# Where the weight tiles start: products of 256 columns with operands at other distances modulo 256 bytes

## The chip, the cores and the metric

The kernel runs on one core of one Trainium2 chip. The metric is the device time of one execution in microseconds. Three timed executions of the kernel before gave 1921.24, 1917.67 and 1925.44, so the median is 1921.24. The execution that the profiler recorded took 1927.16.

## The reference, cut to what matters

Everything is float32, with 256 tokens of x, 256 of a context, and 1024 features. Two blocks run one after the other. The first has a gated FFN (1024 to 2816 and back), attention of two kinds and a second gated FFN:

```python
def swiglu(x, w_gate, w_up, w_down):
    return (jax.nn.silu(x @ w_gate) * (x @ w_up)) @ w_down

h = swiglu(rmsnorm(x, ffn1_pre_g), ffn1_w_gate, ffn1_w_up, ffn1_w_down)
x = x + 0.5 * rmsnorm(h, ffn1_post_g)
qkv = rmsnorm(x, mix_pre_g) @ w_qkv          # then attention of 16 heads
x = x + rmsnorm(concat(o_na, o_dil) @ w_out, mix_post_g)
h = swiglu(rmsnorm(x, ffn2_pre_g), ffn2_w_gate, ffn2_w_up, ffn2_w_down)
x = x + 0.5 * rmsnorm(h, ffn2_post_g)
```

The second block has two layers. Each projects with w_in, mixes in three branches (Fourier, windowed attention, a gated recurrence), and ends with a squared-relu MLP:

```python
y = sum_n(sigmoid(gate_n) * (branch_n @ w_branch[l][n])) @ w_out[l]
x = x + mx[2] * y
x = x + mx[5] * (jnp.square(jax.nn.relu(h2 @ w_ff1[l])) @ w_ff2[l])
```

The first of the two layers works on x and the context together, 512 tokens; the last one updates x alone, 256 tokens.

## The kernel before, in words

The activations are kept with features on the partitions and tokens along the row, so a product takes a weight tile of 128 by 128 as its stationary operand and the activations of 256 tokens (or 512) as its moving one. Products are made to float32 accuracy out of three in the type float32r: each operand is split into a high and a low half, and high by high, high by low and low by high are added in PSUM. So 128 output columns with contraction over 1024 take 8x3 products.

The weights come as a stream of blocks of 128 by 1024, in the order in which TensorE uses them. SyncE loads block n into wr[n % 4]. ACT copies it, rounded, to wh (L451, `make_high`), and DVE or GpSimd subtracts the copy from the original into wl (L468, `make_low`). There are three buffers of wh and three of wl. TensorE reads them in `dense` and `dense_group` (L504, L508, L511) and in `three` (L596 to L604), where L599 is wh by the high half, L602 wh by the low half and L604 wl by the high half. A row of wh or wl holds 1024+64 elements. Where in the row a block starts is `past_line`'s answer for its first tile, in elements of 4 bytes; `Weights.tile` keeps it in `past`, and `halves_of` adds it to each address, for the copy, the subtraction and the product alike.

The buffers wr, wh, wl, X, HH and HL all start at 128 bytes modulo 256. Each tile's columns are 512 bytes further and each k of the activations 1024 or 2048, so within a weight the distance from the weights to the moving operand is one number modulo 256. The moving operands of w_qkv, the gates and ups, w_out, w_ff1_2 and two branches are in HH and HL, at 128; the third branch's are in OHH and OHL, at 128; those of the FFN down products are in NHH and NHL, at 96; those of w_out_2 in the last layer are in Y1, at 96; those of w_ff2_2 there in HID1, at 160. With a start of 16 elements (64 bytes) for HH and 8 (32 bytes) for NHH and Y1 the distance is 192 for all of them: 128-128-64 and 96-128-32 are both -64. `past_line` gives 0 for tiles of 512 columns, for w_in_2 and w_ff2_2, and for all weights of the first of the two layers. There the distance is 0, or 32 for w_ff2_2 in the last layer.

The order of work on TensorE is: FFN1 gate and up to 141 us, its down products to 206, w_qkv to 259, attention, w_out 314 to 337, FFN2 gate and up 341 to 477, its down products to 541; the first layer of the second block to 1409, all but small parts of it with 512 columns; the last layer to the end, with w_branch_2 from 1656 to 1709, w_out_2 to 1734, w_ff1_2 1737 to 1834 and w_ff2_2 after it. In the gate and up products of FFN2 short sums in plain float32 (L678) stand between the products; they belong to a norm of the context.

Of the kernel before, what the change touches and what calls it, by code (L numbers as in the profile page):

```python
# [23 lines left out]
REC_FILLS, OUT_FILLS = ((2, 2, 2, 2, 2, 2, 2), (3, 3, 3, 3, 3, 3, 3)), ((1, 1, 1), (1, 1, 1))  # L24
KB_ = 1024
ARENA = 96 * KB_ + 512
PAST = 16
HALF_D, HALF_T = 65, 130


# [141 lines left out]
def past_line(name, width):  # L172


    if width == 512 or name[0] in ("w_in_2", "w_ff2_2") or name[0].endswith("_2") and name[1] == 0:
        return 0
    return 8 if name[0] in ("ffn1_w_down", "ffn2_w_down", "w_out_2") else PAST


class Weights:  # L180
# [8 lines left out]
    def tile(self, name, k, cols, split=True):  # L189
        width = sum(b - a for a, b in cols)  # L190
        if self.col + width > 1024 or split != self.split:
            self.n, self.col, self.split = self.n + 1, 0, split
            self.kinds.append(split)
            self.past.append(past_line(name, width))
        c = self.col
        self.order.append((self.n, c, name, k, tuple(cols)))
        self.col += width
        self.fill[self.n] = self.col
        end = self.old is not None and self.old.fill[self.n] == self.col
        return self.n, c, self.col, end  # L200
# [3301 lines left out]
```

## Time and profile before

| | us |
|---|---|
| median of three runs | 1921.24 |
| the three runs | 1917.67 to 1925.44 |
| the profiled execution | 1927.16 |
| its span, first to last instruction | 1925.2 |
| TensorE busy in it | 1873.0 |
| weight loads on TensorE | 1661.5 |
| DVE, ACT, GpSimd busy | 1229.9, 944.9, 474.7 |

Products are pipelined: one that is shown as 276 ns long starts 113 ns after the one ahead of it. So the pace of TensorE is read from the starts in the timeline, and its busy time only tells that it had something in work.

### The profile page before, as it was taken

The numbers are of one execution on the slowest core, as the hardware profiler recorded it, in microseconds if no ns is written. First come the engines' busy times: TensorE is split into PE (matmuls) and PEld (weight loads), VectorE is DVE, ScalarE is ACT, GpSimd is POOL, SyncE is SP. The second block draws the span as 40 slices with busy tenths as digits, with TensorE's granted clock in tenths as the row PEclk, the third lists the DMA queues.
The fourth block names the chain that finished last, engine by engine and source line by source line (L and its number), as shares of the span: only waits on it lengthen the run. The fifth ranks groups of instructions, "written<-read, shape, count | busy, mean of one in ns | idle before, by whom it ended". The sixth has DMA issues, their size and how long they took to land.

```text
span 1925.2 us, 31215 instructions
## 1 busy us (share of the span) xinstructions
PE 1873.0 (97%) x12606; PEld 1661.5 (86%) x12606; DVE 1229.9 (64%) x1989; ACT 944.9 (49%) x1508; POOL 474.7 (25%) x328
## 2 busy tenths in 40 slices
PE   8999999999999999999999999999999999999999
PEld 8989988898998888786788888888897998798988
DVE  6888898779857853666663753354377847786410
ACT  6444447655457443426733531233265654765643
POOL 2211022000000000003344354555500000304887
PEclk9999999999999999999999999999999999999999
DMA  8987563576832212221123344466532333154554
GB/s 308 280 256 262 195 221 129 179 229 232 272 130 96 70 47 97 88 66 45 66 97 133 107 168 142 153 218 217 176 101 99 126 128 131 58 177 143 187 193 153
DMA packets 83951, 297.12 MB, mean 154 GB/s; under 512 B 9704, under 2 KB 12912, under 8 KB 83552
## 3 DMA queue, kind: packets, MB, share of 16 engines
q1 hardware_dynamic: 65600, 232.81, 35.9%
q0 software_dynamic: 16592, 58.79, 9.8%
q10 hardware_dynamic: 1616, 3.52, 0.5%
q8 instruction: 100, 1.64, 0.3%
q14 instruction: 43, 0.35, 0.1%
HBM read 294.02 MB, written 2.54 MB: 154 GB/s over the span
## 4 chain that ended last, share of the span: by engine, by line
PE 77%; DVE 12%; ACT 4%; issue 3%; DMA 3%; POOL 1%; DVEq 0%; SPq 0%; ACTq 0%; POOLq 0%
PE ps L604 20%; PE ps L599 20%; PE ps L602 19%; DVE wl L468 4%; PE ps L596 3%; ACT wh L451 2%; DMA wr<-wstream 2%; PE ps L598 1%; PE ps L2180 1%; DMA X<-wmod 1%; PE ps L1379 1%; PE ps L1277 1%; PE ps L1275 1%; PE ps L1280 1%; DVE HH L1133 1%
## 5 line engine op out<-in xcount | busy, mean ns | idle before, releaser
L599 PE MATMUL ps<-HH,wh 128*128 128x256 f32 (+1 forms) x2160 | 700.7, 324 | 4.6 <-ACT wh L451 3.7
L604 PE MATMUL ps<-HH,wl 128*128 128x256 f32 (+1 forms) x2160 | 688.1, 319 | 11.8 <-DVE wl L468 9.6
L602 PE MATMUL ps<-HL,wh 128*128 128x256 f32 (+1 forms) x2160 | 685.7, 317 | 0.0
L451 ACT ACTIVATE wh<-wr 128x1024 fp32r<-128x1024 f32 x440 | 459.6, 1053 | 331.0 <-PE ps L604 227.7
L468 DVE TENSOR_TENSOR wl<-wr,wh 128x1024 fp32r<-128x1024 f32 x301 | 366.9, 1223 | 192.0 <-ACT wh L451 191.5
L604 PEld LDWEIGHTS ps<-HH,wl 128*128 128x128 f32 x2160 | 408.5, 189 | 44.6 <-DVE wl L468 13.3
L599 PEld LDWEIGHTS ps<-HH,wh 128*128 128x128 f32 x2160 | 409.1, 189 | 41.4 <-issue 9.5
L602 PEld LDWEIGHTS ps<-HL,wh 128*128 128x128 f32 x2160 | 409.7, 190 | 30.4 <-issue 2.4
L468 POOL TENSOR_TENSOR wl<-wr,wh 128x1024 fp32r<-128x1024 f32 x139 | 337.1, 2428 | 208.7 <-ACT wh L451 207.7
L1534 POOL TENSOR_TENSOR s<-s,ST 128x512 f32<-128x512 f32 x56 | 57.3, 1039 | 656.9 <-DVE ST L1502 656.6
L1133 DVE CUSTOM_DVE_ANT_0 PROD<-WM,COND 128x1024 f32<-128x1024 f32 x104 | 127.6, 1241 | 1.3
L2940 DVE SCALAR_TENSOR_TENSOR X<-ps,MOD,X 128x256 f32<-128x256 f32 x60 | 26.9, 480 | 139.3 <-PE ps L604 139.0
L1106 POOL DMA_DIRECT2D WM<-wmod x68 | 37.5, 552 | 306.2 <-DVE MOD L1133 306.2
L599 PE MATMUL ps<-HIDH,wh 128*128 128x512 f32 (+1 forms) x272 | 102.6, 377 | 0.0
L604 PE MATMUL ps<-NHH,wl 128*128 128x256 f32 x352 | 99.4, 282 | 3.3 <-DVE wl L468 3.3
L604 PE MATMUL ps<-HIDH,wl 128*128 128x512 f32 (+1 forms) x272 | 102.4, 377 | 0.0
L602 PE MATMUL ps<-HIDL,wh 128*128 128x512 f32 (+1 forms) x272 | 102.4, 377 | 0.0
L599 PE MATMUL ps<-NHH,wh 128*128 128x256 f32 x352 | 98.6, 280 | 0.0
L602 PE MATMUL ps<-NHL,wh 128*128 128x256 f32 x352 | 98.6, 280 | 0.0
L3012 DVE TENSOR_TENSOR tm<-tm,ps 128x512 f32<-128x512 f32 (+1 forms) x64 | 35.4, 553 | 69.6 <-ACT tm L2993 69.6
L596 PE MATMUL ps<-HID,wh 128*128 128x512 f32 x224 | 77.7, 390 | 0.0
L2993 ACT ACTIVATE tm<-ps 128x512 f32<-128x512 f32 (+1 forms) x64 | 31.2, 488 | 81.7 <-PE ps L604 80.2
(314 smaller groups left out, 2968.6 us busy)
## 6 DMA issues: line engine op xcount, KB each, us to landing
wr<-wstream SPq DMA_DIRECT2D x440, 512.0 KB, 3.4
WM<-wmod POOLq DMA_DIRECT2D x68, 512.0 KB, 4.5
X<-wmod POOLq DMA_DIRECT2D x28, 512.0 KB, 6.6
NAB<-naskew POOLq DMA_DIRECT2D x16, 128.0 KB, 7.5
DILB<-dilskew POOLq DMA_DIRECT2D x8, 256.0 KB, 7.4
COND<-cond ACTq DMA_DIRECT2D x2, 1024.0 KB, 4.5
X<-xin SPq DMA_DIRECT2D x4, 256.0 KB, 5.6
HL<-cond ACTq DMA_DIRECT2D x1, 1024.0 KB, 8.2
```

The source lines that it names most:

```text
L451: ins = e.activation(self.halves_of(n, 0, 1024)[0], self.WR[n % NRAW][:, :], ACT.Copy)
L468: ins = e.tensor_tensor(wl, self.WR[n % NRAW][:, :], wh.bitcast(F32), ALU.subtract)
L596: e.matmul(out, wh, beside(xh, xl), start=i == 0, stop=False)
L599: e.matmul(out, wh, xh, start=i == 0, stop=False)
L602: e.matmul(out, wh, xl, start=False, stop=False)
L604: return e.matmul(out, wl, xh, start=False, stop=i == n_k - 1)
L1106: e.dma_start(self.mod_buffer(z, i), src).then_inc(self.mod_sem[i], 16)
L1133: ins = e.tensor_tensor_reduce(out=P, in0=self.mod_buffer(z, i), in1=S, scale=1.0, scalar=0.0, op0=ALU.mult, op1=ALU.add, accum_out=self.M ...
L1534: ins = e.tensor_tensor(sv, sv, bc(st[:, 4:4 + rows], 2, 512 // rows), ALU.mult)
L2940: ins = e.scalar_tensor_tensor(out=self.X[:, d, sl], in0=self.main.item(k)[:, sl], scalar=self.MOD[:, l, mod_i + d, c:c + 1], in1=self.X[: ...
L2993: e.activation(v, self.main.item(key)[:, 0:T], ACT.Relu).then_inc(*self.c("relu").mark((l, f)))
L3012: e.tensor_tensor(v, v, self.main.item(key)[:, 0:T], ALU.mult).then_inc(*self.c("sqr").mark((l, f)))
```

## The change

The constant PAST, 16 elements, becomes a table by the weight's name, and the exception for three names goes into it.

```diff
-PAST = 16
+PAST = dict(ffn1_w_gate=48, ffn1_w_up=48, ffn1_w_down=40, w_qkv=24, w_out=24, ffn2_w_gate=8, ffn2_w_up=8,
+            ffn2_w_down=0, w_branch_2=32, w_out_2=8, w_ff1_2=40)
@@ def past_line(name, width):
     if width == 512 or name[0] in ("w_in_2", "w_ff2_2") or name[0].endswith("_2") and name[1] == 0:
         return 0
-    return 8 if name[0] in ("ffn1_w_down", "ffn2_w_down", "w_out_2") else PAST
+    return PAST[name[0]]
```

With the places of the moving operands the distances become:

| weight | start before, after (bytes) | moving operand at | distance before, after |
|---|---|---|---|
| ffn1 gate, up | 64, 192 | 128 | 192, 64 |
| ffn1 down | 32, 160 | 96 | 192, 64 |
| w_qkv (q and k), w_out | 64, 96 | 128 | 192, 160 |
| ffn2 gate, up | 64, 32 | 128 | 192, 224 |
| ffn2 down | 32, 0 | 96 | 192, 224 |
| w_branch_2, last layer | 64, 128 | 128 | 192, 128 |
| w_out_2, last layer | 32, 32 | 96 | 192, 192 |
| w_ff1_2, last layer | 64, 160 | 128 | 192, 96 |

## Rows read from the trace of the kernel before

**Rows 1.** The page: busy time by engine, granted clock in 40 slices, last chain.

```profile
PE 1873.0 (97%) x12606; PEld 1661.5 (86%) x12606; DVE 1229.9 (64%) x1989; ACT 944.9 (49%) x1508; POOL 474.7 (25%) x328
...
PEclk9999999999999999999999999999999999999999
...
PE 77%; DVE 12%; ACT 4%; issue 3%; DMA 3%; POOL 1%; DVEq 0%; SPq 0%; ACTq 0%; POOLq 0%
```

**Rows 2.** Timeline of TensorE, FFN2 gate and up: start, duration (us), instruction.

```profile
383.17 0.28 PE L604 MATMUL ps<-HH,wl 128*128 128x256 f32 x1
...
385.89 0.28 PE L604 MATMUL ps<-HH,wl 128*128 128x256 f32 x1
```

**Rows 3.** Timeline of TensorE, FFN2 down.

```profile
484.54 0.28 PE L602 MATMUL ps<-NHL,wh 128*128 128x256 f32 x1
...
540.49 0.28 PE L604 MATMUL ps<-NHH,wl 128*128 128x256 f32 x1
```

**Rows 4.** Timeline of TensorE, w_in_2 in the last layer.

```profile
1551.92 0.28 PE L602 MATMUL ps<-HL,wh 128*128 128x256 f32 x1
...
1571.84 0.28 PE L604 MATMUL ps<-HH,wl 128*128 128x256 f32 x1
```

**Rows 5.** Timeline of TensorE, last output of w_ff2_2.

```profile
1910.99 0.28 PE L599 MATMUL ps<-HID,wh 128*128 128x256 f32 x1
...
1921.84 0.28 PE L599 MATMUL ps<-HID,wh 128*128 128x256 f32 x1
```

**Rows 6.** Timeline of TensorE, w_ff2_2 in the first layer, 512 columns.

```profile
1199.82 0.39 PE L599 MATMUL ps<-HIDH,wh 128*128 128x512 f32 x1
...
1201.86 0.39 PE L599 MATMUL ps<-HIDH,wh 128*128 128x512 f32 x1
```

**Rows 7.** Timeline of TensorE, FFN2 gate and up, around an L678 sum.

```profile
392.09 0.60 PE L678 MATMUL ps<-tm,CT 128*128 128x256 f32 x2
...
393.11 0.28 PE L604 MATMUL ps<-HH,wl 128*128 128x256 f32 x1
```

**Rows 8.** Windows on slow stretches: length, PE busy (count), clock, DMA, GB/s; sums: all 18, then by weight.

```profile
sum 294.69, PE 294.69; mean PE 16.37
...
sum 49.82, PE 49.82; mean PE 12.46
...
155.19:197.23 42.04, 42.04 (x359) 1.00 0.78 263
...
sum 16.26, PE 16.26; mean PE 5.42
...
317.54:337.09 19.55, 19.55 (x169) 1.00 0.74 265
...
386.55:392.09 5.54, 5.54 (x50) 1.00 0.55 164
...
sum 27.33, PE 27.33; mean PE 5.47
...
484.54:540.61 56.07, 56.07 (x479) 1.00 0.78 263
...
1686.18:1691.60 5.42, 5.42 (x49) 1.00 0.30 100
...
sum 78.20, PE 78.20; mean PE 39.10
```

**Rows 9.** L468 on DVE, FFN1 gate and up, then down: min/median/max ns.

```profile
L468 DVE TENSOR_TENSOR wl<-wr,wh x39: 1205/1221/1228, 19.0 to 136.9; 128x1024 fp32r<-128x1024 f32 x39
...
L468 DVE TENSOR_TENSOR wl<-wr,wh x23: 1216/1222/1228, 141.0 to 204.6; 128x1024 fp32r<-128x1024 f32 x23
```

**Rows 10.** Waits of the weight loads, 354 to 477 us: total, times, longest.

```profile
PEld ps L604 <- DVE wl L468: 5.5, 6, 1.1
```

**Rows 11.** Groups of instructions, 1747 to 1834 us: count, busy us, mean ns, idle before.

```profile
L468 POOL TENSOR_TENSOR wl<-wr,wh 128x1024 fp32r<-128x1024 f32 x29 | 69.7, 2408 | 86.5 <-ACT wh L451 86.5
```

**Rows 12.** Window on FFN1 gate and up, TensorE alone, columns as in rows 8.

```profile
20.00:141.00 121.00, 115.36 (x963) 1.00 0.92 277
```

## The prediction

> **What bounds the kernel now.** I read the page's busy line and its chain first [rows 1]: TensorE is busy 97% of the span and holds 77% of the chain that ended last, so in most stages its pace is the pace of the kernel. The change moves weight tiles in memory and adds or removes no instruction, so the question is whether the pace of one product depends on the place of its operands. A product's duration doesn't tell it, since products overlap; the distance from one start to the next in the timeline does. Where TensorE waits for nothing, four spacings are to be seen, and D is the distance in bytes from the weights to the moving operand, modulo 256:
>
> With D=192 there is a fast pace: in the second FFN's gate and up products, 24 products start between 383.17 and 385.89 us, 113.3 ns each [rows 2]. With the same D there is a slow one: in that FFN's down products, 475 between 484.54 and 540.49, 117.8 ns each [rows 3]. With D=0, in the last layer's w_in_2, 166 between 1551.92 and 1571.84, 120.0 ns each [rows 4]. With D=32, in the last outputs of w_ff2_2, 93 between 1910.99 and 1921.84, 116.7 ns each [rows 5]. Products of 512 columns at D=0 take 226.7 ns (9 between 1199.82 and 1201.86 [rows 6]), which is twice 113.3: there the distance costs nothing, and 113.3 looks like the floor for 256 columns. The clock isn't it: the page grants nine tenths or more of full speed in each slice of the span [rows 1], and 1.00, the level of 2.4 GHz, in the slow stretches [rows 8].
>
> So place matters, and at D=192 the pace has two values that hold for long stretches. What ends one is a break in the stream: behind the L678 sum that follows the product at 385.89 the pace is slow from 386.55 on [rows 2, 8], behind the same sum at 392.09 it is fast from 393.11 on [rows 7]. The slow one isn't bound to a weight.
>
> How much of it there is: 18 stretches of slow pace, found by going through the starts and shown by their sum, hold 294.69 us (the first sum of [rows 8]). A slow product costs 117.8-113.3=4.45 ns over the floor, 3.78% of its time, so all slow stretches together cost 11.1 us. That is the most that the floor can give back. They hold 294.69/0.11778=2502 products of the 4800 whose D changes (by the code, three products for each 128 columns of output and each k: gate and up 2x44x8x3=2112, down 2x8x22x3=1056, w_qkv's q and k 16x8x3=384, w_out 192, w_branch_2 in the last layer 3x8x4x3=288, w_ff1_2 in the last layer 32x8x3=768). The other 2298 are taken as fast. w_out_2 keeps 192, and products of 512 columns, w_in_2 and w_ff2_2 keep their places.
>
> **The change part by part.** No instruction, wait or DMA is added, removed or moved past a queue. The copies to wh (L451) and the subtractions to wl (L468) write the same bytes at another offset. Their cost I take at nothing: at offsets of 64 bytes in FFN1 and 32 in its down stage the median subtraction is 1221 and 1222 ns [rows 9].
>
> What is left is the pace at each new D, and no trace shows 64, 96, 128, 160 or 224. The bounds for each are the ends of the rows: 113.3 below and 120.0 above. Between them I choose by distance on the circle of 256 bytes, since the known rows fall with it: 120.0 at 0, 116.7 at 32, 113.3 or 117.8 at 64 (192 is 64 the other way round).
>
> First, w_ff1_2 (96), w_qkv and w_out (160) and w_branch_2 (128) come to lie further apart than 64, where I take the fast pace throughout. Their slow stretches now [rows 8]: w_ff1_2 78.20 us (two stretches), w_out 19.55, w_qkv 16.26 (three stretches), w_branch_2 5.42; together 119.43 us, times 3.78% is -4.5 us. Bounds: -4.5, or 1632 products at 120.0, which is 10.9-4.5=+6.4.
>
> Second, FFN1 goes to 64, the same distance as 192. I take no difference. Bounds: its slow stretches [rows 8], gate and up 49.82 (four of them) and down 42.04, gone: -3.5 us; all of its 1584 products at 120.0: +7.1.
>
> Third, FFN2 goes to 224, the distance of D=32, so 116.7 for all. Its down stage is slow now over 56.07 us [rows 8], 476 products that would gain 1.1 ns each, and 52 at the floor lose 3.3: -0.35 us. Its gate and up stage has 27.33 us slow (one stretch ahead of 361 us, and four of 47 products behind L678), 232 products, and 824 products at the floor that would lose 3.3 ns each, +2.7, less 0.3. Part of that is hidden: from 434 us on TensorE runs 40 to 90 fast products and then waits for DVE's subtraction, in the stage six waits of the weight load with 5.5 us in all, the longest 1.1 [rows 10]. A product later by 3.3 ns takes 0.3 us off such a wait. What is open to view are the fast stretches between the L678 sums and ahead of them, some 350 products: +1.2-0.3=+0.9. With down: +0.55. Bounds: -3.2 (slow stretches gone) and +7.4 (all at 120.0).
>
> Sum: -4.5+0+0.55=-4.0 us. Made against the profiled execution, span 1925.2 and 1927.16 in all, that is 1923.2. The three timed runs lie lower, 1917.67 to 1925.44 with the median at 1921.24, and the sum is the same there: **1917.2 us**. Their spread of 7.8 us is of the size of all slow stretches together.
>
> Does anything take the gain back? In w_ff1_2 GpSimd makes the low half, 29 times 2408 ns in 87 us, and what it waits for is ACT's copy [rows 11]; a block of 8x3 products at the floor takes 2.72 us against 2.83 now, still above 2.41, so it holds. In FFN1 the DMA engines are busy 92% of 20 to 141 us [rows 12], and a faster TensorE there would mostly meet its waits sooner.
>
> A sentence of the Trainium skill speaks against all of this: the page "TensorE: Matmul & The Clock Gate", Part 2, says that the moving operand and the weight load have independent read ports, so that loading the next weights takes no bandwidth from the running product. By it no D would matter and the change would be worth 0; the rows at D=0 and D=192 don't agree (120.0 against 113.3 ns), so it stays a rival only. The same page gives columns/2.4 + 2.5 ns between starts at full clock, by which 256 columns would take 109.2 ns and the floor would lie 4.1 ns lower, an estimate that no row here shows.
>
> **The rivals.** *All new distances are fast.* For it: the fast pace exists at D=192 next to the slow one, so a slightly better distance may never fall into the slow one. Against: the nearest row to 224 is 116.7. It would give 11.1 us, less what FFN1's transfers take back (half of its gate and up share of 1.9 us), 10.1: 1911 us.
>
> *The distance decides nothing beyond 0 and 32.* For it: at one D the pace changes behind a break [rows 7], so it may be the break alone that decides, and the new kernel draws the same kind of lot again, some stages better and some worse. Against: D=0 shows no fast stretch. 1921, give or take 3 us. If the tiles didn't move as the diff says, the time would be this too.
>
> *A new distance meets like D=0.* Two streams that read at different speeds may meet again at a distance that isn't near on the circle; then it is 120.0 there. For it: D=192 is slow in half of its products, so 64 is no safe distance. Against: the fall from 0 to 32. If it holds for FFN2's 1584 products alone, +7.4 us, 1928. If it holds for all 4800: 576.0 us against 294.7+2298x0.1133=555.1 now, +20.9, 1942. It decides from a mean of 117.65 ns over the 4800 (115.65 now), which is +9.6 us, 0.5%.
>
> **How the numbers follow.** The forecast has 0.38, all fast 0.20, the lot of breaks 0.30, a distance like 0 has 0.12. A measurement of this kernel tells about 0.5%, 9.6 us, from no change. Faster by more needs nearly all of the 11.1 us: most of the second case and a little of the first, 0.17. Slower by more needs the last case beyond FFN2, with a little of the third: 0.08. The rest, 0.75, lies within. The range reaches from a little below the all-fast time, 1909.5, to 1926, which takes in the poor draws of the breaks and leaves most of the last case out.
>
> **What would show it right or wrong.** The count of instructions on TensorE must be as before. Spacings in the timeline, with waits left out: 113.3 in w_ff1_2 from 1747 us on would show the first step right, anything at 117.8 or above wrong. FFN2's down products at 116.7 would show the circle right; at 113.3 it is wrong to the good, at 120.0 to the bad. FFN1 should show both paces again. If TensorE's slow stretches are gone and the span hasn't fallen with them, the idle time ahead of L604 and L599 must have grown.

## The result, and the profile after

The changed kernel takes 1926.87 us (median of 20 runs, 1924.23 to 1929.78) against 1918.26 for the kernel before, timed beside it (20 runs, 1913.63 to 1925.44). The ratio is 1.0039, with a 95% interval of 1.0031 to 1.0046: 0.4% slower. The prediction had 1917.2 and a range up to 1926.0. That the time would stay within 0.5% was right. The direction was wrong, and so was the range, by 0.9 us.

The recorded execution has a span of 1923.2 us, which is shorter than the 1925.2 of the kernel before [rows 1]. So the two recorded executions can't be set against each other as wholes, and the first experiment below shows why. The page of the changed kernel, its busy line and its chain:

```profile
PE 1879.4 (98%) x12606; PEld 1670.3 (87%) x12606; DVE 1229.0 (64%) x1989; ACT 945.2 (49%) x1508; POOL 474.9 (25%) x328
...
PE 83%; DVE 9%; ACT 4%; issue 3%; DMA 1%; POOL 1%; DVEq 0%; SPq 0%; ACTq 0%; POOLq 0%
```

TensorE has the same 12606 products, is busy 6.4 us longer, and holds 83% of the last chain, where it held 77%. In these two chains, what was wait before is now product. Its timeline shows the pace at three of the new distances (start, duration, instruction; one line further down in the code than before). First FFN1's down products, D=64, then FFN2's, D=224, then w_ff1_2, D=96:

```profile
160.06 0.28 PE L603 MATMUL ps<-NHL,wh 128*128 128x256 f32 x1
...
189.98 0.28 PE L600 MATMUL ps<-NHH,wh 128*128 128x256 f32 x1
...
500.12 0.28 PE L605 MATMUL ps<-NHH,wl 128*128 128x256 f32 x1
...
529.94 0.28 PE L605 MATMUL ps<-NHH,wl 128*128 128x256 f32 x1
...
1790.06 0.28 PE L603 MATMUL ps<-HL,wh 128*128 128x256 f32 x1
...
1819.93 0.29 PE L603 MATMUL ps<-HL,wh 128*128 128x256 f32 x1
```

They are 254, 252 and 249 products, 117.8, 118.3 and 120.0 ns each. The floor of [rows 2], 113.3 ns, is at none of them, and w_ff1_2 at 96 bytes runs as the products at distance 0 do [rows 4]. FFN1's gate and up, at 64 too, were the exception: 48 spacings from 57.16 us on and 46 from 108.75 us on are 113.3 ns, the other stretches 117.8.

### The profile page after: what moved, and what is told of

Its sections match the earlier page's. It is cut to its first block, busy times and chain, and to the rows that moved or that the text cites. A ratio compares the mean times of both kernels' runs of the same rounds, so it can differ in the third digit from the quotient of the medians.

```text
span 1923.2 us, 31215 instructions
## 1 busy us (share of the span) xinstructions
PE 1879.4 (98%) x12606; PEld 1670.3 (87%) x12606; DVE 1229.0 (64%) x1989; ACT 945.2 (49%) x1508; POOL 474.9 (25%) x328
## 4 chain that ended last, share of the span: by engine, by line
PE 83%; DVE 9%; ACT 4%; issue 3%; DMA 1%; POOL 1%; DVEq 0%; SPq 0%; ACTq 0%; POOLq 0%
PE ps L605 21%; PE ps L600 21%; PE ps L603 21%; DVE wl L469 3%; PE ps L597 3%; ACT wh L452 2%; PE ps L599 1%; PE ps L2181 1%; PE ps L1380 1%; PE ps L1278 1%; PE ps L1276 1%; PE ps L1281 1%; PE ps L1420 1%; PE ps L1399 1%; PE ps L505 1%
```

## The experiments

Each is the kernel before or the changed one with the edit that is shown, or a kernel of products alone. Of a table only the entries that change are shown. "Over before" and each ratio go by runs of the kernel before that were timed beside the run in question, with medians of 1917.59 to 1919.70 us. Lengths of stages below are from the first start to the last in the timeline.

**The kernel before, recorded once more.** No edit.

> The kernel before, recorded once more. Theory (the pace at D=192 is a lot drawn behind each break, and the first recorded execution, 1927.16 us against a median of 1918.26, drew badly): the span comes out about 9 us shorter than 1925.2, and the stretches at 117.8 ns hold under 100 us in place of 294.69. Rival (the 9 us are something else, DMA or waits): the stretches at 117.8 ns hold about 295 us again, in the same places, and the difference is in the waits.

It took 1921.65 us with a span of 1919.7, 5.5 under the first record. Its stretches at 117.8 ns, found in the same way as those of [rows 8], in a view by windows (length, PE busy and count; the sum of all 17):

```profile
sum 138.54, PE 138.54; mean PE 8.15
```

That is 138.5 us in place of 294.69, and the 156.2 us fewer give 156.2 x 3.78% = 5.9 us. They went mostly where the prediction had counted most: FFN2's down stage is 61.9 us long in place of 64.0 (all but a few of its products at the floor), and w_ff1_2's 92.8 in place of 95.3. Here is w_ff1_2, where 264 products start 113.3 ns apart:

```profile
1790.06 0.28 PE L599 MATMUL ps<-HH,wh 128*128 128x256 f32 x1
...
1819.98 0.28 PE L599 MATMUL ps<-HH,wh 128*128 128x256 f32 x1
```

So at D=192 the pace of a stage differs from one execution to the next, and the first record was one with much of it slow. The theory holds in kind; the span is 5.5 us shorter in place of the 9 expected, and the slow stretches hold 138.5 us where under 100 were expected.

**Sixteen distances, nothing else running.** Products alone, six tries at each distance. The stream on TensorE, with three buffers each of wh and wl in turn:

```python
at = (256 - d) % 256 // 4                  # d: the distance in bytes
...
c = at + 128 * k
h, l = wh[:, c:c + 128], wl[:, c:c + 128]
e.matmul(out, h, HH[:, k, 0:256], start=k == 0, stop=False)
e.matmul(out, h, HL[:, k, 0:256], start=False, stop=False)
...
last = e.matmul(out, l, HH[:, k, 0:256], start=False, stop=k == 7)
```

> A kernel that leaves the whole computation out: real weights and activations, split in the same way, and then products of 256 columns in the order high by high, high by low, low by high without any other load, 96 at each of 16 distances (0 to 240 bytes in steps of 16), each distance six times, behind three kinds of break (TensorE waits for DVE ahead of a wh product, ahead of a wl product, or two plain float32 sums stand between). Theory (the pace is a property of the distance, and the new ones are all worse than 192 at its best): 120.0 ns at 0, about 117.8 at 64, 117.5 to 118.3 at 160 and 224, 118.6 at 128, 119.9 at 96, each whatever the break, and 113.3 at 192 behind some breaks and 117.8 behind others. Rival (circle of the prediction): the same pace at 32 and 224, at 64 and 192, at 96 and 160. Rival (contention with other engines makes the slow pace): all distances but 0 at 113.3 here, where DVE, ACT and DMA rest.

Measured, the spacing of the products from the 31st of each try on (ns; two values where the tries differ, with their number):

```
  0 120.0      64 117.8            128 118.7 (5), 120.0 (1)   192 113.3 (5), 117.8 (1)
 16 120.0 (3), 117.3 (3)  80 118.1 144 120.0                  208 117.8 (4), 118.3 (2)
 32 116.7 (5), 117.8 (1)  96 120.0 160 117.3 (2), 118.7 (4)   224 118.3
 48 116.7     112 120.0 (3), 118.3 (2), 116.7 (1)  176 118.7  240 118.3
```

The paces of the changed kernel are here: 117.8 at 64, 118.3 at 224, 120.0 at 96, 118.7 at 128. No DVE, ACT or DMA work ran beside the products that were counted, so contention with other engines isn't needed for these paces. The circle of the prediction falls: 32 and 224 differ (116.7 and 118.3), 96 and 160 differ (120.0 and 117.3 or 118.7), and 128, the furthest, is worse than 32. Among the sixteen only 192 reaches the floor.

**What meets what.** Products alone again, three tries each, with the distance of wh and wl, the place of both (x0), and the two widths varied.

```python
ah, al, x0 = (x0 - dh) % 256 // 4, (x0 - dl) % 256 // 4, x0 // 4    # dh, dl: distances of wh and wl
...
ch, cl = ah + 128 * k, al + 128 * k
h, l = wh[:, ch:ch + cols], wl[:, cl:cl + cols]
xh, xl = HH[:, k, x0:x0 + width], HL[:, k, x0:x0 + width]
```

> A kernel that leaves the whole computation out, as the one for the 16 distances: products of 256 columns only, 96 in each case, three breaks. Cases: distances 176 to 204 in steps of 4; distance 192 with both operands moved by 32 to 160 bytes; wh at distance 0 with wl at 192 and the other way; at distance 0 a stationary operand of 64 and of 96 columns; at distances 0, 96 and 192 moving operands of 272 to 384 columns. Theory (the stream of the weight load and that of the product meet in the memory at the same time, and only the difference of their starts counts): 192 keeps 113.3 wherever both lie; with one of wh and wl at distance 0 the mean lies between 113.3 and 120.0; with 64 columns the load is over in half the time and the pace is 113.3 or less at distance 0; with more moving columns the load has slack, and from some width on all three distances give one pace, 113.3 x columns/256. Rival (a fixed cost of a start address, of one operand alone): moving both changes the pace, and the width doesn't make the distances equal.

With both operands moved by 32 to 160 bytes at distance 192, 13 of 15 tries are at 113.3 and two at 117.8, as one of three is without the move: the difference counts, not the place. With one of wh and wl at 0 and the other at 192 it is 117.8 (122.3 once). At distance 0 a stationary operand of 64 columns brings the floor back; 60 products between these two starts, 113.4 ns each:

```profile
222.57 0.28 PE L114 MATMUL ps<-HH,wl 128*64 128x256 f32 x1
...
229.38 0.28 PE L114 MATMUL ps<-HH,wl 128*64 128x256 f32 x1
```

With 96 columns it is 116.0, with 128 it is 120.0. The loads themselves, of 128 and of 64 columns, last 188 and 134 ns:

```profile
L110 PEld LDWEIGHTS ps<-HH,wh 128*128 128x128 f32 x2592 | 488.5, 188 | 42.8 <-DVE T L77 42.1
...
L110 PEld LDWEIGHTS ps<-HH,wh 128*64 128x64 f32 x96 | 12.9, 134 | 1.6 <-DVE T L77 1.5
```

Those of 96 columns last 161, so 32 columns more are 27 ns more. By this, an estimate, 128 columns are read in some 108 ns, about as long as a product of 256 columns takes at the floor. Wider moving operands give the load more time, and here the result is mixed. At 272 columns the distances 0 and 96 give 125.3 to 126.7 against 123.3 at 192. At 288, 0 and 96 give 131.7 and 192 gives 133.3. At 320 all three give 146.7. At 384, though, 96 gives 176.7 each time, 0 gives 173.3, and 192 gives 173.3, 174.7 and 176.7. The expected pace of 113.3 x columns/256 didn't come either: 320 columns would be 141.7 and 384 would be 170.0. So a shorter load takes the loss at distance 0 away, which fits that load and product hinder each other; a wider product doesn't simply do so. The 512-column products of [rows 6] are at twice the floor, but no distance other than theirs was tried.

**All 64 distances.** Products alone, in steps of 4 bytes, four tries each.

```python
CASES = [(d, d, 0, 128, 256) for d in range(0, 256, 4)]
```

> A kernel that leaves the whole computation out, as the two before it: products of 256 columns only, 72 at each of the 64 distances that are multiples of 4 bytes, behind four breaks (TensorE waits ahead of the first, second or third product, or two plain float32 sums). Theory: few distances reach the floor of 113.3 ns; 180 and 204 do behind each break, 192 behind some, and all others lie at 116.7 to 122. Rival (nearness on the circle of 256 bytes decides): the pace falls evenly from 0 to 128 and rises again, and 180 is no better than 176 or 184.

All four tries reach 113.3 at 180 and 204 only, three of four at 168 and 192, two at 52, one at 64 and 76. All others lie between 115.6 (248) and 122.3 (148). The neighbours 176, 180 and 184, 60 products in each pair of rows of the timeline, 118.8, 113.3 and 118.3 ns:

```profile
477.73 0.28 PE L112 MATMUL ps<-HH,wl 128*128 128x256 f32 x1
...
484.86 0.28 PE L112 MATMUL ps<-HH,wl 128*128 128x256 f32 x1
...
487.84 0.28 PE L112 MATMUL ps<-HH,wl 128*128 128x256 f32 x1
...
494.64 0.28 PE L112 MATMUL ps<-HH,wl 128*128 128x256 f32 x1
...
497.60 0.28 PE L112 MATMUL ps<-HH,wl 128*128 128x256 f32 x1
...
504.70 0.28 PE L112 MATMUL ps<-HH,wl 128*128 128x256 f32 x1
```

Four bytes decide. No curve over the distance could have been drawn from the three points that the trace before had.

**All at distance 0.**

```diff
-    return 8 if name[0] in ("ffn1_w_down", "ffn2_w_down", "w_out_2") else PAST
+    return 56 if name[0] in ("ffn1_w_down", "ffn2_w_down", "w_out_2") else 0
```

> The kernel before with the same weights at distance 0 in place of 192 (start 0, and 56 for the down products and w_out_2). Theory (each weight costs its products times the pace at its distance, but for FFN1's gate and up, which the transfers hold): 120.0 ns everywhere; outside FFN1's gate and up 3744 products at 120.0 in place of some 114.5, +21 us, less what waits take back: 1934 to 1939 us, 0.8 to 1.1% over before. Rival (the loss of the changed kernel isn't in the pace of products): no more than the changed kernel's 1927.

1932.53 us, ratio 1.0067 (1.0050 to 1.0083), 12.8 us over before and more than the changed kernel's 8.6. The order is as the pace says, and the size is below the 21 us of pace; the 8 us between are put down to waits, which wasn't shown by itself. It also came out under the lower end that was expected, 1934.

**One part alone, on the kernel before.** First w_ff1_2 at 96:

```diff
+    if name[0] == "w_ff1_2":
+        return 40
```

> The kernel before with w_ff1_2 alone at 96 (start 40). Theory: its stage takes 96.8 us as in the changed kernel, in place of 92.8 to 95.3, so +1.5 to +4 us in all, 0.1 to 0.2%. Rival (something later in the kernel takes it back): the stage is longer and the time is the same within 1 us.

1923.07 us, ratio 1.0019 (1.0008 to 1.0030), +3.4 us; its stage 95.3 us, against 92.8 and 95.3 in the two records of before and 96.8 in the changed kernel. The pace was 120.0 ns as in the changed kernel; what is missing to 96.8 is a stretch of 16 or so products 213 ns apart, at a granted clock of 0.50 (the level of 1.2 GHz), which the changed kernel and both records of before have between 1761 and 1768 us, behind a wait of 2.2 us, and which this record hasn't behind the same wait. Like for like, 96 costs that stage 4.0 us against the second record of before (96.8 and 92.8). Then FFN2 at 224:

```diff
+    if name[0].startswith("ffn2"):
+        return 0 if name[0] == "ffn2_w_down" else 8
```

> The kernel before with FFN2's weights alone at 224 (start 8, down 0). Theory: gate and up 135.3 us in place of 133.3 to 135.2, down 64.0 in place of 61.9, +2 to +4 us, 0.1 to 0.2%. Rival (waits for DVE hide the slower products): under +1 us.

1922.36 us, ratio 1.0017 (1.0007 to 1.0028), +3.0 us; gate and up 135.4 us, down 64.0. Then FFN1 at 64:

```diff
+    if name[0].startswith("ffn1"):
+        return 40 if name[0] == "ffn1_w_down" else 48
```

> The kernel before with FFN1's weights alone at 64 (start 48, down 40). Theory (gate and up are held by the transfers, so only down's 528 products at 117.8 count): gate and up between 133 and 138 us as in every kernel so far, down 63.6 to 64.4 in place of 61.9 to 64.4, in the time +0 to +2 us. Rival (FFN1 makes a large part of the changed kernel's loss): +3 us or more.

1920.21 us, ratio 1.0005 (0.9991 to 1.0019), +0.9 us, which can't be told from nothing; gate and up 134.5 us, down 63.6. In time the three intervals reach from 1.5 to 5.8 us, from 1.3 to 5.4 and from -1.7 to 3.6, so the order of the parts isn't certain.

**One part taken back, on the changed kernel.** w_ff1_2 back at 192, twice:

```diff
-w_ff1_2=40
+w_ff1_2=16
```

> The changed kernel with w_ff1_2 alone back at 192 (start 16 in place of 40). Theory (w_ff1_2's pace at 96, 119.9 ns, is the largest part of the loss): its 768 products go to 113.3 to 117.8, so 1.6 to 5.0 us less than the changed kernel, 1922 to 1925 us; against the kernel before still slower by 0.2 to 0.3%. Rival (the loss is made in the FFNs of the first block): under 1.5 us of gain.

> The changed kernel with w_ff1_2 back at 192, once more. Its stage was 4.0 us shorter the first time and yet its time (1928.28) not under the changed kernel's 1926.87. Theory (FFN1's gate and up stage happened to be long, 137.7 us, from waits for transfers, and hid it): the median comes to 1922 to 1925 us and FFN1's gate and up to 133 to 136. Rival (the part given back at w_ff1_2 is lost elsewhere each time, by the new places in memory): 1927 to 1929 again with FFN1's gate and up at 137.

The two are the same kernel, timed in two sets. The first time 1928.28 us, ratio to before 1.0050 (1.0032 to 1.0068), no gain over the changed kernel although the stage was 92.8 us in place of 96.8. The second time 1923.05, ratio 1.0022 (1.0013 to 1.0031): 3.8 us less than the changed kernel by the medians, 3.3 by the ratios. The intervals of the two sets don't overlap although the kernel is one, so the same kernel can come out 0.28% apart in two sets, more than an interval tells. Differences of 0.1 to 0.2% between kernels that had one set each have to be read with that. In the first one's record FFN1's gate and up took 137.7 us, with ACT waiting for the weight stream; the waits of ACT in the first 145 us, in the changed kernel and then in that one (total us, times, longest):

```profile
ACT wh L452 <- DMA wr<-wstream: 10.4, 10, 2.7
```

```profile
ACT wh L452 <- DMA wr<-wstream: 23.4, 16, 3.2
```

The stage is 133.8 us in the changed kernel and 135.4 in the second try of the edit. In the one recorded execution the longer stage hid the gain; what the other five did was not seen.

FFN1 taken back, and in another kernel FFN2 taken back:

```diff
-ffn1_w_gate=48, ffn1_w_up=48, ffn1_w_down=40
+ffn1_w_gate=16, ffn1_w_up=16, ffn1_w_down=8
-ffn2_w_gate=8, ffn2_w_up=8, ffn2_w_down=0
+ffn2_w_gate=16, ffn2_w_up=16, ffn2_w_down=8
```

> The changed kernel with FFN1's gate, up and down back at 192. Theory (each weight's loss is the pace at its new distance, 117.8 at 64 against 113.3 to 117.8 at 192): in the trace FFN1's down stage shortens from 63.6 by 0 to 2 us and the gate and up stage's pace falls while its waits grow; in the time 0 to 4 us less than the changed kernel. Rival (FFN1 is held by the transfers): no more than 1 us.

> The changed kernel with FFN2's gate, up and down back at 192. Theory: 1584 products at 118.3 (distance 224) go to between 113.3 and 117.8, down to about 62 us from 64.0, and with what the waits of gate and up take back 2 to 5 us less than the changed kernel. Rival (gate and up are held by DVE, and down by nothing): only down's part, 2 us.

FFN1: 1928.68 us, 1.0053 (1.0035 to 1.0071), no gain; the pace of gate and up fell from 117.4 to 114.7 ns and the stage took 137.1 us all the same, with 21.9 us of it in starts over 130 ns apart where the changed kernel has 16.5. FFN2: 1924.17 us, 1.0034 (1.0023 to 1.0046), 2.7 us less by the medians and 1.0 by the ratios; gate and up 133.6 us. Its down stage was still 64.0 us long there, a draw of 117.8 at D=192.

**Better places.** w_in_2 of the last layer and w_ff2_2 (start 24) at 192 too, then w_in_2 alone, whose edit this is:

```diff
-    if width == 512 or name[0] in ("w_in_2", "w_ff2_2") or name[0].endswith("_2") and name[1] == 0:
+    if width == 512 or name[0] == "w_ff2_2" or name[0].endswith("_2") and name[1] == 0:
```

> The kernel before with the last layer's w_in_2 (0 before) and w_ff2_2 (32 before) at 192 too: start 16 and 24 in place of 0. Theory (192 is the best distance of those seen, 0 the worst): 930 products of w_in_2 go from 120.0 to between 113.3 and 117.8, and w_ff2_2's from 117.8 to the same, 2 to 7.5 us less than before, 0.1 to 0.4% faster. Rival (those stages are held by DVE and ACT, so TensorE's pace doesn't count): the same time as before within 1 us, with longer waits in the last layer.

> The kernel before with the last layer's w_in_2 alone at 192 (start 16 in place of 0), w_ff2_2 left at 32: with w_ff2_2 at 192 too its last stage took 90.0 us in place of 88.4 and w_in_2's 204.1 in place of 207.7. Theory: 3.5 us less in w_in_2's stage and nothing given back, 0.1 to 0.2% faster than before, about 1914.5 us. Rival (the time of an execution is set by the lots in the FFNs, and 3.5 us can't be told): within 0.1%.

Both: 1919.39 us, 1.0004 (0.9991 to 1.0017). w_in_2's part of the last layer shortened from 207.7 to 204.1 us, w_ff2_2's grew from 88.7 to 90.3. Its wide products take their moving operand from two places, but why they got slower isn't shown. w_in_2 alone: 1915.99 us, 0.9992 (0.9977 to 1.0006), its part 203.7 us. The 4.0 us are in the trace and can't be told in the time.

Then all weights of the change and w_in_2 at 204 (w_ff2_2 stays at 32), and the same at 180, where 13 and 5 become 19 and 11:

```diff
-    return 8 if name[0] in ("ffn1_w_down", "ffn2_w_down", "w_out_2") else PAST
+    return 5 if name[0] in ("ffn1_w_down", "ffn2_w_down", "w_out_2") else 13
```

> The kernel before with distance 204 in place of 192 for all (start 13, and 5 for the down products and w_out_2), and the last layer's w_in_2 at 204 too. Theory (at 204 the floor of 113.3 ns holds behind each break): w_in_2's stage falls from 207.7 to about 202, no stretches at 117.8 in the FFNs, 1908 to 1913 us, 0.3 to 0.5% under before. Rival (the breaks of the real kernel, with waits for wl in the stream, are others than those tried): stretches at 117.8 or so remain and the gain is w_in_2's 3.5 us alone.

> The kernel before with distance 180 for all (start 19, and 11 for the down products and w_out_2) and the last layer's w_in_2 at 180 too. At 180 each of seven tries so far gave 113.3 ns; at 204, with as many, w_ff1_2 in the real kernel still ran at 118.5. Theory (180 holds the floor in the real kernel): w_ff1_2's stage 92.7, both down stages 61.9 and 62.5, w_in_2's 203 or less; 1911 to 1915 us. Rival (the breaks in the real kernel bring other phases, as at 204): some stages at 117 to 120 and 1914 to 1917 us.

At 204: 1915.57 us, 0.9977 (0.9963 to 0.9991). At 180: **1914.18 us, 0.9964 (0.9949 to 0.9980)**, 0.4% faster than before and 0.7% faster than the changed kernel by the medians. Some of that is w_in_2's, whose distance changed too, and each of the two kernels was timed in one set only. The timeline of w_ff1_2 tells them apart; at 204 there are 249 products of 120.0 ns between these starts,

```profile
1790.07 0.28 PE L602 MATMUL ps<-HL,wh 128*128 128x256 f32 x1
...
1819.95 0.28 PE L602 MATMUL ps<-HL,wh 128*128 128x256 f32 x1
```

and at 180 there are 264 of 113.3 ns between these:

```profile
1790.04 0.28 PE L599 MATMUL ps<-HH,wh 128*128 128x256 f32 x1
...
1819.96 0.28 PE L599 MATMUL ps<-HH,wh 128*128 128x256 f32 x1
```

In products alone 204 held the floor in each of seven tries, and the real kernel still found a pace at which it doesn't. 180 held it in seven tries too, and in the real kernel nearly everywhere: down stages 65.0 (with 5.1 us of waits) and 61.9 us, w_out 22.4, w_in_2's part 203.6, w_ff1_2 92.9. But in FFN1's gate and up 92 spacings between 45.55 and 56.59 us are 120.0 ns, at full clock (columns as in [rows 8]):

```profile
45.60:56.60 11.00, 11.00 (x94) 1.00 1.01 231
```

So none of 192, 204 and 180 holds the floor behind every break of the real kernel; 180 leaves it least, in the records at hand.

## Why the prediction was wrong

The mean spacing of products in each stage, starts over 130 ns apart left out (ns), and the stage's length (us):

| stage | before, first record | before, second | changed |
|---|---|---|---|
| FFN1 gate, up | 115.4, 133.9 | 115.2, 134.7 | 117.4, 133.8 |
| FFN1 down | 116.5, 64.4 | 113.6, 62.6 | 117.8, 63.6 |
| w_qkv, q and k | 115.3, 48.7 | 114.3, 49.3 | 118.1, 48.0 |
| w_out | 117.4, 22.9 | 117.3, 22.9 | 117.5, 23.0 |
| FFN2 gate, up | 114.6, 135.1 | 115.1, 135.2 | 118.3, 135.3 |
| FFN2 down | 117.4, 64.0 | 113.4, 61.9 | 118.3, 64.0 |
| w_branch_2 (192 in a row) | 114.4, 23.0 | 117.8, 23.6 | 118.6, 23.7 |
| w_ff1_2 | 117.4, 95.3 | 113.5, 92.8 | 119.9, 96.8 |

*What bounds the kernel* held. Product spacing is what moved, the instructions are the same, and the order of the kernels by pace is their order by time: over these stages the mean spacing is 113.7 ns with all at 180, 115.9 and 114.6 in the two records at 192, 118.3 with the new table and 119.9 with all at 0.

*The floor* held: in no run did 20 weight products of 256 columns in a row have a mean spacing below 113.3 ns. The page of the Trainium skill "TensorE: Matmul & The Clock Gate" gives 2.5 ns over columns/2.4 in Part 2, for a product by itself, by which an estimate here is 109.2 ns; no run shows that for these products. Its sentence on independent read ports, which would have made the change worth nothing, isn't borne out either: with the load halved the loss at distance 0 is gone (120.0 to 113.4 ns), so load and product hinder each other here.

*The choice by distance on the circle* is the step that failed. It was drawn through three distances, 0, 32 and 64, and four bytes are enough to leave a floor. It set 96, 128 and 160 to 113.3 where they run at 119.9, 118.6 and 117.5 to 118.1, and 224 to 116.7 where it runs at 118.3. Term by term: w_ff1_2, w_qkv, w_out and w_branch_2 were to give 4.5 us, 2.96 of it (78.20 x 3.78%) at w_ff1_2, and w_ff1_2 alone cost 3.4; FFN2 was to cost 0.55 and cost 3.0; FFN1 was to cost nothing and cost 0.9, within its interval of nothing. These three sum to 7.3 of the measured 8.6 us, which is closer than their intervals, 2 to 3 us to each side of every one, can promise. The rest, 1.3, falls to w_qkv, w_out and w_branch_2, which weren't tried alone.

*The size of what could be won* failed beside it. The prediction took 294.69 us of slow stretches from one record and carried the sum over to the median, though that record lay 8.9 us above the median of 20 runs (1927.16 against 1918.26). The second record, itself 3.4 us above that median, has 138.5 us. Its slow stretches are worth 138.54 x 3.78% = 5.2 us. So a run near the median, by this estimate, has less than half of the 11.1 us left to give, and a distance that is slow each time costs the more against it. The spread of the three runs was noted in the prediction as of the same size, and not used.

*What the waits hide* was right in kind and too small. Against the second record the changed kernel's products are 16.6 us slower over these eight stages (their excess over the floor is 22.5 us against 5.9), and the stages are together 5.0 us longer. The starts over 130 ns apart lost 11.6 us. FFN1's gate and up show it best: 2 ns slower each, and not longer, with the DMA engines busy 92% of the stretch as in [rows 12]. In FFN2's gate and up, where 0.9 us was to be left in view, the six waits of the weight load fell from 5.5 us [rows 10] to 4.6.

That stage looks no longer, 135.3 us against 135.1 and 135.2, but waits aren't all of it. In both records of before, behind waits of 1.1 and 1.0 us, 16 or 17 of its products start 213 ns apart, at half the clock. The changed kernel's record, behind waits of 0.5 and 1.0 us, has none of them. The windows, before and changed (columns as in [rows 8], the clock before the DMA share):

```profile
379.10:382.60 3.50, 3.50 (x17) 0.52 0.60 187
...
376.80:383.00 6.20, 6.13 (x50) 1.00 0.51 172
```

The stretch costs 17 x (213 - 113) = 1.7 us. It doesn't come each time: of the other kernels whose FFN2 is at 192, five records are without it, three of them behind waits of 1.1 and 1.0 us too. Without it the stage is 133.3 to 133.9 us at 192 and 135.3 to 135.4 at 224, so the new distance costs about 2 us there, and the waits hid less than the two records of before suggest. The prediction's check of the clock, in 40 slices of 48 us, couldn't show so short a stretch.

*The copies at no cost* held: DVE is busy 1229.0 us against 1229.9, ACT 945.2 against 944.9.

*The rivals.* "A new distance meets like D=0" was the one that came true, at 0.12, with 96 at 120.0 ns. Its point of decision, a mean of 117.65 ns over the 4800 products, was passed: the stages' means weighted by their products give 118.3. The time went up by 8.6 us only, under the mark of 9.6, for the rival's price too left out what the waits take back. "The lot of breaks" described D=192 rightly, and D=64 too: FFN1 showed both paces again, as the prediction asked of it, though more of the slow one. It described 96 and 224 wrongly, which have one pace each in every stretch and try.

## What to carry to other kernels

Where a weight load takes as long as the product that covers it (128 columns against 256 here), the distance between the two operands in memory sets the pace, 113.3 to 122 ns, or the two paces between which a break chooses, and neither nearness nor roundness tells which: measure all distances in a kernel of products alone, and then the best few in the real one, for seven good tries at 204 and at 180 didn't promise the floor there. Products of 512 columns ran at twice the floor at distance 0, where those of 256 columns lose 6.7 ns; their other distances are open. Where the pace of a stage can differ from run to run, one recorded execution is one draw: ask how far its time lies from the median before taking a term from it, look in the stage itself for a stretch at half the clock, and count what the waits next to a slower engine will take back. And where the same kernel comes out 0.28% apart in two sets, time what matters in more than one.

## What the runs showed of the hardware that was not expected

At D=192 the same stream runs at 113.3 or 117.8 ns from start to start, and can hold either for tens of microseconds. It changes behind a break, and also, more rarely, where a few starts come up to 15 ns late without one: at 98.2 us in the second record the spacings go from 113 over 119, 128 and 115 to 118 ns and stay there. In products alone it was 113.3 in 10 of 13 tries with neither operand moved, and behind the same kind of break both paces came. Both were seen at full granted clock: 1.00 in the slow stretches of [rows 8] and in 383.10 to 386.00 us, the stretch of [rows 2]. The distances that reach 113.3 at least once form two rows with steps of 12 bytes (52, 64, 76 and 168, 180, 192, 204). No run here gives a reason for that, and where in the memory or the array the two streams meet stays open too. Open is also what chooses between the two paces.
